# A transformer kernel: the four conditioning pieces of layer 1 that lay in norms, placed in the two projections

## Chip, cores and metric

The kernel runs on one NeuronCore of a Trainium2 chip. The metric is the time of one execution on the device in microseconds (us). The engines are TensorE (PE), VectorE (DVE), ScalarE (ACT), GpSimd (POOL) and SyncE (SP), which issues the weight transfers.

## The reference

Four layers over 256 tokens of width 1024, all in fp32. Layers 0 and 1 are conditioned: six vectors of 1024 per layer (shift, scale and gate of the mixer; shift, scale and gate of the feed-forward part) come from one product of the conditioning input with a weight of 1024 x 6144. Each is made for two streams, the latent tokens (`x`, conditioned by `c`) and the context tokens (`ctx`, conditioned by `c_ctx`):

```python
for l in range(DEPTH):
    mod = (jax.nn.silu(c) @ ada_w[l] + ada_b[l])[:, None, :]
    mod_c = (jax.nn.silu(c_ctx) @ ada_w[l] + ada_b[l])[None, None, :]
    sh1, sc1, g1, sh2, sc2, g2 = jnp.split(mod, 6, axis=-1)
    h = x * (1.0 + sc1) + sh1
    ...
    x = layer_norm(ALPHA * x + g1 * y, ln1_g[l], ln1_b[l])
    x = layer_norm(ALPHA * x + g2 * swiglu(x * (1.0 + sc2) + sh2, ffn_w_in[l], ffn_w_out[l]), ln2_g[l], ln2_b[l])
```

`y` is the mixer of the layer (attention and pooling in layer 0; differential attention and a convolution in layer 1). Layer 0 runs its output projection, norm, feed-forward part and second norm for both streams, layer 1 for the latent tokens alone. Layers 2 and 3 (mLSTM and RG-LRU mixers, cross attention, feed-forward with retrieved experts) have no conditioning and are not touched by the change.

## The kernel before

**Stages.** The program is a list of stages that all engines enter in turn: an engine leaves a stage with a drain and an increment, and `enter` waits until the others have left the stages before. For the conditioned layers the order is `ada0`, `modulate0`, `project0`, `attend0`, `pool`, then `out00`, `hidden00` (context) and `out01`, `hidden01` (latent), then `modulate1`, `project1`, `attend1`, `subln`, `out11`, `hidden11`. The `out` stages multiply by the output weight and end in a norm; the `hidden` stages are the feed-forward parts and end in a norm too. The hidden stages round their weights into a high and a low part (`w_split`, made by ACT at L1497 and DVE at L1887) and multiply three times.

**The ring.** All weights stream in blocks of 128 x 1024 fp32 (512 KB) through a ring of `R = 6` slots. `WEIGHTS` is the one list of the blocks in order; SP issues them (L531), waiting before block i until PE has used block i - 6 (`block_used`). A stage finds its blocks by `first_block`.

**A conditioning piece** is one of the six vectors of a layer, `KD = 8` blocks. `ada_block` (L698 to L704) multiplies a block: four matmuls of 32 columns, one for each quarter of the vector, side by side in the array; `ada_sum` is the bank in which a piece is summed, alternating between two. When the eight blocks of a piece are used, `keep_ada` on ACT (L1383 to L1386) copies the sum out, `ada_turn` on PE (L707 to L713) turns it into columns with two small matmuls, and `biased` on DVE (L1810 to L1822) adds the bias into `mod`, with 1 added to the two scale pieces. Before the first block of a piece, PE waits until the piece two before it is biased (`ada_out`), since the bank is the same.

**Where the pieces lie.** Pieces 0 and 1 of layer 0 are made in `ada0`. The projection puts conditioning blocks between its products: `ADA_AFTER[l][n]` says how many follow product n. In layer 0 that is three after each of ten products and two after the eleventh, the 32 blocks of pieces 2 to 5. In layer 1 it is one after each of the first 16 of 22 products, pieces 4 and 5. Pieces 0 to 3 of layer 1 are made in the norms at the end of `out00`, `hidden00`, `out01` and `hidden01`: there PE, after the matmuls for mean (L953) and variance (L959), runs the eight blocks of a piece (`ada_in_norm`, L715), while ACT and DVE finish the norm: root (L1389), reciprocal (L1685), scaling (L1861), shift (L1478) and, in the `out` stages, the modulated input of the hidden stage and its split (L1474, L1870, L1875). The piece is copied at the end of ACT's norm, turned between mean and variance of the next norm, and biased there by DVE; piece 3 is turned and biased at the head of `project1`.

**The projection** (`project_early`). PE runs for each n: product n (L806 and L809; 16 matmuls for 256 or 512 tokens, each counted as it appears in the trace), the conditioning blocks of n (L703), the turns of the pieces that were completed after product n - 1 (L712), and in layer 0 the head mean of n - 1 (L818) and the rotary partner of n - 2 (L829); in layer 1 the partner of n - 5, and two means for the convolution near the end (L836). ACT copies each product out and, in layer 0, squares it and takes the root; DVE normalizes and rotates in layer 0, and in layer 1 rotates and runs the 31 convolution taps. `BIASED_AT[l]` says after which of DVE's steps a piece is biased, and `pieces_after` when ACT copies one.

The expression that sets the mix of blocks in a projection (`project_weights`):

```python
for n in range(n_products):
    blocks.append((f"project{l}", tensor, 1, n))
    if ADA_AFTER[l][n]:
        blocks.append((f"project{l}", f"ada{l}", ADA_AFTER[l][n], at))
        at += ADA_AFTER[l][n]
```

Of the kernel before, what the change touches and what calls it, by code (L numbers as in the profile page):

```python
# [36 lines left out]
KD = D // P  # L37
# [24 lines left out]
QUARTER = D // 4  # L62
# [96 lines left out]
def project_weights(l, tensor, n_products):  # L159

    blocks, at = [], ADA_FIRST[l]
    for n in range(n_products):
        blocks.append((f"project{l}", tensor, 1, n))
        if ADA_AFTER[l][n]:
            blocks.append((f"project{l}", f"ada{l}", ADA_AFTER[l][n], at))
            at += ADA_AFTER[l][n]
    return blocks


ADA_AFTER = {0: [3] * 10 + [2, 0], 1: [1] * 16 + [0] * 6}  # L170
ADA_FIRST = {0: 2 * KD, 1: 4 * KD}
BIASED_AT = {0: {3: (2,), 6: (3,), 7: (4,)}, 1: {6: (4,), 11: (5,)}}
ADA_IN_NORM = ["out00", "hidden00", "out01", "hidden01"]
# [7 lines left out]
def pieces_after(l, n):  # L181
# [6 lines left out]
           ("out00", "ab_out", 8), ("ada1_0", "ada1", KD, 0), ("hidden00", "ffn0", 0), ("ada1_1", "ada1", KD, KD),  # L188
           ("out01", "ab_out", 8), ("ada1_2", "ada1", KD, 2 * KD), ("hidden01", "ffn0", 0), ("ada1_3", "ada1", KD, 3 * KD),
           ] + project_weights(1, "cd_in", 22) + [("out11", "cd_out", 8), ("hidden11", "ffn1", 0),  # L190
# [100 lines left out]
def program(nc, a, out, spread_rows):  # L291
    ctx = ExitStack()
    with ctx:
# [152 lines left out]

        def ada_sum(l, n):
            return ps[:, (2, 6)[l] + n % 2, 0:QUARTER]

        def ada_columns(l, n):  # L450
            return ps[:, (2, 6)[l] + n % 2, QUARTER:QUARTER + 2 * KD]
# [233 lines left out]
        def _(pe):  # L685
            place = RingPlace()
# [11 lines left out]
            def ada_block(l, n, k, blk):  # L698

                if k == 0 and n >= 2:  # L700
                    pe.wait_ge(ada_out, 6 * l + n - 1)
                for q in range(4):
                    last = mm(ada_sum(l, n)[32 * q:32 * (q + 1), :], cond_wide[:, k, :],  # L703
                              ring[:, blk[0], q * QUARTER:(q + 1) * QUARTER], start=(k == 0), stop=(k == KD - 1))  # L704
                last.then_inc(block_used, 1)
# [9 lines left out]

            def ada_in_norm(n):

                for k in range(KD):
                    place.steps(pe, 1, 1, lambda _, par, b: (wait_filled(b[0]), ada_block(1, n, k, b[0])))
# [70 lines left out]
            def project_early(l):  # L790
# [49 lines left out]
                if l == 1:  # L840
                    ada_turn(1, 3)
                turns = []
                for n in range(len(tiles)):
                    place.steps(pe, 1, 1, lambda _, par, b: product(n, b[0]))
                    at = ADA_FIRST[l] + sum(ADA_AFTER[l][:n])
                    for i in range(at, at + ADA_AFTER[l][n]):
                        place.steps(pe, 1, 1, lambda _, par, b: (wait_filled(b[0]), ada_block(l, i // KD, i % KD, b[0])))
                    for i in turns:
                        ada_turn(l, i)
# [98 lines left out]
            def norm(name):  # L948

                piece = ADA_IN_NORM.index(name) if name in ADA_IN_NORM else None  # L950
# [4 lines left out]
                if piece:  # L955
                    ada_turn(1, piece - 1)
# [6 lines left out]
                if piece is not None:  # L963
                    ada_in_norm(piece)
# [307 lines left out]
        def _(act):  # L1272
# [70 lines left out]
            def project_early(l):  # L1343
# [4 lines left out]
                for n, (j, _, nt, _) in enumerate(project_tiles(l)):  # L1348
# [22 lines left out]
                    for i in pieces_after(l, n):  # L1371
                        last = (i + 1) * KD - 1 - ADA_FIRST[l]
                        keep_ada(l, i, product_block(l, n) + 2 + last - sum(ADA_AFTER[l][:n]))
# [84 lines left out]
            def norm(name, s, ln, k12, follow=None):  # L1458
# [24 lines left out]
                if name in ADA_IN_NORM:  # L1483
                    n = ADA_IN_NORM.index(name)
                    keep_ada(1, n, first_block(f"ada1_{n}") + KD)
# [186 lines left out]
        def _(dve):  # L1672
# [37 lines left out]
            def project_early(l):  # L1710

                enter(dve, f"project{l}")
                if l == 1:
                    biased(1, 3)
                for i in range(len(ROPE[l])):
# [11 lines left out]
                    for n in BIASED_AT[l].get(i, ()):  # L1727
                        biased(l, n)
                if l == 0:
                    n_sq[0] += len(ROPE[0])  # L1730
                    rotate(l, len(ROPE[0]) - 1)
                    biased(0, 5)
# [116 lines left out]
            def norm(name, s, ln, k12, follow=None):  # L1849
# [6 lines left out]
                if name in ADA_IN_NORM[1:]:  # L1856
                    biased(1, ADA_IN_NORM.index(name) - 1)
# [615 lines left out]
```

## Time and profile before

| what | value |
|---|---|
| median of 3 runs | 3460.69 us |
| the runs | 3453.43, 3460.69, 3462.86 us |
| the profiled execution, its time | 3451.77 us |
| its span | 3450.1 us |
| mean granted clock of PE, of full speed | 0.96 |
| busy share PE, DVE, ACT, POOL | 92%, 60%, 36%, 3% |
| moved from memory | 543.92 MB read, mean 168 GB/s over the span |
| projection of layer 0, PE | 43.0 to 158.7 us |
| projection of layer 1, PE | 781.1 to 923.0 us |

The span is the time between first and last instruction in the trace; the execution's own time has 1.7 us more around it. In rows of the timeline the columns are start (us), length (us), engine, line, operation, output and inputs, count of merged instructions, and in brackets the idle time before and what ended it. Lengths of PE rows overlap slightly, so a piece of work is best measured from its start to the start of the next row. An fp32 matmul appears as two records.

### The profile page before, as it was taken

How to read it: one execution, taken by the hardware profiler on the slowest of the kernel's cores; microseconds unless marked ns; L12 is line 12 of the kernel's file. 1: busy time of each engine (PE TensorE's matmuls, PEld its weight loads, DVE VectorE, ACT ScalarE, POOL GpSimd, SP SyncE). 2: the span in 40 equal slices, each digit the busy share in tenths (PEclk: the TensorE clock that was granted, in tenths of full speed). 3: DMA queues.
4: the chain of work that ended last, by engine and by line, in shares of the span. 5: the costliest groups of instructions: out<-in, count | busy, mean ns of one | idle time of the engine just before them, and what ended most of it. 6: DMA issues, size and time to landing. Idle time of an engine off the chain costs nothing.

```text
span 3450.1 us, 52714 instructions
## 1 busy us (share of the span) xinstructions
PE 3162.0 (92%) x20312; PEld 2725.2 (79%) x20312; DVE 2083.7 (60%) x3709; ACT 1246.9 (36%) x1886; POOL 111.5 (3%) x135
## 2 busy tenths in 40 slices
PE   6978998999878999688999999999789899999998
PEld 2547987985758978477998999887678899999886
DVE  1474554553445540459995666784539996666686
ACT  1143443441224421122553444433422454444433
POOL 0110000000000000003000000000002100000000
PEclk9999999999989999799999999999889999999999
DMA  7504554545114533033556655674224466666663
GB/s 270 180 1 166 188 183 170 184 176 194 69 49 153 185 133 128 16 119 123 197 219 225 222 204 206 225 241 140 85 92 145 155 227 238 206 221 206 212 241 138
DMA packets 190525, 580.70 MB, mean 168 GB/s; under 512 B 16768, under 2 KB 61824, under 8 KB 185504
## 3 DMA queue, kind: packets, MB, share of 16 engines
q1 hardware_dynamic: 185120, 541.04, 44.9%
q10 hardware_dynamic: 4608, 33.56, 2.3%
q0 software_dynamic: 640, 4.00, 0.3%
q8 instruction: 101, 1.65, 0.2%
q14 instruction: 56, 0.46, 0.0%
HBM read 543.92 MB, written 34.60 MB: 168 GB/s over the span
## 4 chain that ended last, share of the span: by engine, by line
PE 82%; DVE 11%; ACT 4%; DMA 1%; issue 1%; DVEq 0%; ACTq 0%; SPq 0%; POOL 0%; POOLq 0%
PE ps L930 29%; PE ps L971 26%; PE ps L921 4%; PE ps L806 4%; PE ps L764 4%; PE ps L1172 3%; PE ps L809 2%; DVE w_split L2075 1%; PE ps L900 1%; PE ps L959 1%; ACT arena L1425 1%; PE ps L953 1%; PE ps L885 1%; DVE arena L1685 1%; PE ps L1137 1%
## 5 line engine op out<-in xcount | busy, mean ns | idle before, releaser
L930 PE MATMUL ps<-x_split,w_split 128*128 128x256 f32 x9312 | 1190.6, 286 | 72.5 <-DVE w_split L2075 39.8
L930 PEld LDWEIGHTS ps<-x_split,w_split 128*128 128x128 f32 x9312 | 1165.7, 194 | 97.0 <-issue 77.6
L971 PE MATMUL ps<-w_split,h_split 128*128 128x512 f32 x3864 | 916.6, 391 | 4.9 <-DVE w_split L2075 4.9
L971 PEld LDWEIGHTS ps<-w_split,h_split 128*128 128x128 f32 x3864 | 714.2, 189 | 146.4 <-issue 5.3
L2075 DVE TENSOR_TENSOR w_split<-ring,w_split 128x1024 fp32r<-128x1024 f32 x512 | 627.9, 1227 | 325.6 <-ACT w_split L1532 324.8
L1532 ACT ACTIVATE w_split<-ring 128x1024 fp32r<-128x1024 f32 x512 | 541.2, 1058 | 390.1 <-PE ps L971 352.1
L1887 DVE TENSOR_TENSOR w_split<-ring,w_split 128x1024 fp32r<-128x1024 f32 x198 | 242.3, 1226 | 237.8 <-ACT w_split L1497 237.8
L1497 ACT ACTIVATE w_split<-ring 128x1024 fp32r<-128x1024 f32 x198 | 209.1, 1059 | 330.4 <-PE ps L930 227.1
L1540 ACT ACTIVATE arena<-ps 128x256 f32<-128x256 f32 (+1 forms) x256 | 98.6, 385 | 460.8 <-PE ps L930 459.0
L921 PE MATMUL ps<-arena,ring 128*128 128x256 f32 (+1 forms) x672 | 154.1, 393 | 7.4 <-DVEq L1679 4.5
L806 PE MATMUL ps<-arena,ring 128*128 128x512 f32 (+1 forms) x416 | 154.8, 526 | 4.8 <-ACTq L1278 4.8
L921 PEld LDWEIGHTS ps<-arena,ring 128*128 128x128 f32 (+1 forms) x672 | 132.8, 199 | 29.1 <-issue 8.0
L764 PE MATMUL ps<-x,ring 128*128 128x256 f32 (+1 forms) x608 | 133.6, 382 | 6.3 <-ACTq L1278 6.3
L1137 PE MATMUL ps<-x,ring 128*128 128x256 f32 x512 | 119.6, 388 | 18.6 <-DVEq L1679 18.6
L806 PEld LDWEIGHTS ps<-arena,ring 128*128 128x128 f32 x416 | 81.0, 197 | 68.8 <-issue 63.7
L764 PEld LDWEIGHTS ps<-x,ring 128*128 128x128 f32 (+1 forms) x608 | 109.2, 180 | 30.1 <-issue 7.1
L1685 DVE RECIPROCAL arena<-arena 128x256 f32<-128x256 f32 (+2 forms) x26 | 63.1, 2429 | 108.7 <-ACT arena L1389 108.7
L1137 PEld LDWEIGHTS ps<-x,ring 128*128 128x128 f32 x512 | 97.4, 196 | 32.0 <-issue 19.4
L2204 DVE TENSOR_TENSOR h_split<-x,h_split 128x256 fp32r<-128x256 f32 x256 | 108.9, 425 | 8.8
L2197 DVE TENSOR_TENSOR x<-arena 128x256 f32<-128x256 f32 x256 | 107.5, 420 | 8.7 <-DMA arena<-spread_rows 8.7
L2180 DVE TENSOR_TENSOR arena<-arena,x 128x3072 bf16<-128x3072 bf16 x64 | 112.0, 1749 | 0.0
L1172 PE MATMUL ps<-res,arena 128*128 128x128 bf16 x1536 | 108.2, 227 | 0.4 <-DVE arena L2180 0.4
(264 smaller groups left out, 2439.4 us busy)
## 6 DMA issues: line engine op xcount, KB each, us to landing
ring<-in_peer_u SPq DMA_DIRECT2D x256, 512.0 KB, 3.5
ring<-in_peer_v SPq DMA_DIRECT2D x256, 512.0 KB, 4.3
ring<-in_ffn_in SPq DMA_DIRECT2D x132, 512.0 KB, 3.2
ring<-in_ada SPq DMA_DIRECT2D x96, 512.0 KB, 4.4
ring<-in_ffn_out SPq DMA_DIRECT2D x66, 512.0 KB, 3.2
spread_rows<-arena ACTq DMA_DIRECT2D x32, 1024.0 KB, 3.9
arena<-spread_rows SPq DMA_DIRECT2D x20, 1536.0 KB, 8.7
ring<-in_pq SPq DMA_DIRECT2D x32, 512.0 KB, 3.2
```

The lines of the kernel that those rows point to most:

```text
L764: last = mm(pair[0:width, par, 0:nt], w[:, k, :], src[:, k, t0:t0 + nt], start=(k == 0), stop=(k == KD - 1))
L806: last = mm(pair[:, n % 2, 0:nt], w[:, k, :], hT[:, k, t0:t0 + nt], start=(k == 0), stop=(k == KD - 1))
L921: last = mm(wide[:, m, :], ring[0:rows, blk[0], m * P:(m + 1) * P], rhs, start=(first and m % 2 == 0), stop=final, skip_group_check=True)
L930: last = mm(dst, w_split[:, w, wp, at:at + P], rhs[rp], start=(first and i == 0), stop=(final and i == 2), skip_group_check=shared)
L971: last = mm(ps[:, 2 * r + c, :], h_split[:, ph, hp, r * P:(r + 1) * P], w_split[:, b[3], wp, c * 512:(c + 1) * 512], start=(first and i == ...
L1137: last = mm(single[:, m % 2, 0:T], ring[:, b[0], k * P:(k + 1) * P], x[:, LAT, k, :], start=(k == 0), stop=(k == KD - 1))
L1172: last = mm(ps[:, bank, u * KEYS:(u + 1) * KEYS], hot_w[:, s % 2, c, :, 4 * half + u], hot_i[:, s % 2, 4 * half + u, :], start=(c == 0), s ...
L1497: f(w_split[:, w, 0, :], ring[:, slot, :], ACT.Copy).then_inc(w_high, 1)
L1532: f(w_split[:, w, 0, :], ring[:, slot, :], ACT.Copy).then_inc(w_high, 1)
L1887: v.tensor_tensor(w_split[:, w, 1, :], ring[:, slot, :], w_split[:, w, 0, :].bitcast(F32), ALU.subtract).then_inc(w_low, 1)
L2075: v.tensor_tensor(w_split[:, w, 1, :], ring[:, slot, :], w_split[:, w, 0, :].bitcast(F32), ALU.subtract).then_inc(w_low, 1)
L2180: v.tensor_tensor(hot_w[:, b], hot_j[:, b].unsqueeze(1).to_broadcast([P, 3, KEYS, GROUP]), weight3[:, :, at].unsqueeze(2).to_broadcast([P, ...
```

## The change

The list `ADA_AFTER` of layer 0 gets 48 blocks (four after each of eight products, then 5, 5 and 6), which are pieces 2 to 5 of layer 0 and pieces 0 and 1 of layer 1; that of layer 1 gets 32 (two after each of the first 16 products), pieces 2 to 5. Nothing of the conditioning stands in the norms any more, neither blocks nor turns, copies or biases. The number of blocks stays 96. Pieces 0 and 1 of layer 1 use banks 2 and 3, like those of layer 0; the later ones 6 and 7. `BIASED_AT` holds pieces numbered through both layers (layer 1 begins at 6) and gives their places on DVE; pieces 0 and 1 of layer 1 are biased at the end of the projection of layer 0.

```diff
--- before.py
+++ after.py
@@ -161,16 +161,16 @@
     blocks, at = [], ADA_FIRST[l]
     for n in range(n_products):
         blocks.append((f"project{l}", tensor, 1, n))
-        if ADA_AFTER[l][n]:
-            blocks.append((f"project{l}", f"ada{l}", ADA_AFTER[l][n], at))
-            at += ADA_AFTER[l][n]
+        for _ in range(ADA_AFTER[l][n]):
+            blocks.append((f"project{l}", f"ada{at // (6 * KD)}", 1, at % (6 * KD)))
+            at += 1
     return blocks
 
 
-ADA_AFTER = {0: [3] * 10 + [2, 0], 1: [1] * 16 + [0] * 6}
-ADA_FIRST = {0: 2 * KD, 1: 4 * KD}
-BIASED_AT = {0: {3: (2,), 6: (3,), 7: (4,)}, 1: {6: (4,), 11: (5,)}}
-ADA_IN_NORM = ["out00", "hidden00", "out01", "hidden01"]
+ADA_AFTER = {0: [4] * 8 + [5, 5, 6, 0], 1: [2] * 16 + [0] * 6}
+ADA_FIRST = {0: 2 * KD, 1: 8 * KD}
+BIASED_AT = {0: {1: 2, 3: 3, 5: 4, 7: 5}, 1: {0: 8, 3: 9, 7: 10, 11: 11}}
+
 
 
 def product_block(l, n):
@@ -185,9 +185,7 @@
 
 
 WEIGHTS = [("ada0", "ada0", 2 * KD, 0)] + project_weights(0, "ab_in", 12) + [
-           ("out00", "ab_out", 8), ("ada1_0", "ada1", KD, 0), ("hidden00", "ffn0", 0), ("ada1_1", "ada1", KD, KD),
-           ("out01", "ab_out", 8), ("ada1_2", "ada1", KD, 2 * KD), ("hidden01", "ffn0", 0), ("ada1_3", "ada1", KD, 3 * KD),
-           ] + project_weights(1, "cd_in", 22) + [("out11", "cd_out", 8), ("hidden11", "ffn1", 0),
+           ("out00", "ab_out", 8), ("hidden00", "ffn0", 0), ("out01", "ab_out", 8), ("hidden01", "ffn0", 0)] + project_weights(1, "cd_in", 22) + [("out11", "cd_out", 8), ("hidden11", "ffn1", 0),
            ("project2", "ml_in", 26), ("project2", "kv0", 4), ("out21", "ml_out", 8), ("hidden2", "peer0", 0),
            ("project3", "rg_in_r", 16), ("project3", "rg_in_q", 2), ("project3", "kv1", 4),
            ("out31", "rg_out_q", 2), ("out31", "rg_out_r", NRB), ("hidden3", "peer1", 0)]
@@ -444,11 +442,14 @@
         stored = sem("stored")
         bank_ready, rows_kept, back_ready = sem("bank_ready"), sem("rows_kept"), sem("back_ready")
 
+        def ada_bank(l, n):
+            return (6 if (l, n) >= (1, 2) else 2) + n % 2
+
         def ada_sum(l, n):
-            return ps[:, (2, 6)[l] + n % 2, 0:QUARTER]
+            return ps[:, ada_bank(l, n), 0:QUARTER]
 
         def ada_columns(l, n):
-            return ps[:, (2, 6)[l] + n % 2, QUARTER:QUARTER + 2 * KD]
+            return ps[:, ada_bank(l, n), QUARTER:QUARTER + 2 * KD]
 
         def rg_sum(g):
             bank = (0, 1, 2, 3, 6, 7, 0, 1)[g // 2]
@@ -697,7 +698,7 @@
 
             def ada_block(l, n, k, blk):
 
-                if k == 0 and n >= 2:
+                if k == 0:
                     pe.wait_ge(ada_out, 6 * l + n - 1)
                 for q in range(4):
                     last = mm(ada_sum(l, n)[32 * q:32 * (q + 1), :], cond_wide[:, k, :],
@@ -712,11 +713,6 @@
                     last = mm(ada_columns(l, n)[:, 8 * c:8 * (c + 1)], ada_row[:, at:at + P], const("pick"),
                               start=True, stop=True)
                 last.then_inc(ada_turned, 1)
-
-            def ada_in_norm(n):
-
-                for k in range(KD):
-                    place.steps(pe, 1, 1, lambda _, par, b: (wait_filled(b[0]), ada_block(1, n, k, b[0])))
 
             def ada(l):
 
@@ -837,16 +833,14 @@
                                   start=(k == 0), stop=(k == 1))
                     last.then_inc(conv_p, 1)
 
-                if l == 1:
-                    ada_turn(1, 3)
                 turns = []
                 for n in range(len(tiles)):
                     place.steps(pe, 1, 1, lambda _, par, b: product(n, b[0]))
                     at = ADA_FIRST[l] + sum(ADA_AFTER[l][:n])
                     for i in range(at, at + ADA_AFTER[l][n]):
-                        place.steps(pe, 1, 1, lambda _, par, b: (wait_filled(b[0]), ada_block(l, i // KD, i % KD, b[0])))
+                        place.steps(pe, 1, 1, lambda _, par, b: (wait_filled(b[0]), ada_block(i // (6 * KD), i // KD % 6, i % KD, b[0])))
                     for i in turns:
-                        ada_turn(l, i)
+                        ada_turn(i // 6, i % 6)
                     turns = pieces_after(l, n)
                     if l == 1 and n >= len(tiles) - 4 and n < len(tiles) - 2:
                         conv_mean(n - (len(tiles) - 4))
@@ -947,21 +941,16 @@
 
             def norm(name):
 
-                piece = ADA_IN_NORM.index(name) if name in ADA_IN_NORM else None
                 for k in range(KD):
                     pe.wait_ge(res_ready, KD * n_ln[0] + k + 1)
                     last = mm(pair[:, 0, 0:T], const("mean_d"), res[:, k, :], start=(k == 0), stop=(k == KD - 1))
                 last.then_inc(ln_mean, 1)
-                if piece:
-                    ada_turn(1, piece - 1)
                 for k in range(KD):
                     pe.wait_ge(ln_squared, 4 * n_ln[0] + k // 2 + 1)
                     last = mm(pair[:, 1, 0:T], const("mean_d"), work[:, k * T:(k + 1) * T],
                               start=(k == 0), stop=(k == KD - 1))
                 last.then_inc(ln_var, 1)
                 n_ln[0] += 1
-                if piece is not None:
-                    ada_in_norm(piece)
 
             def token_rows(ph, b, first, final):
 
@@ -1370,7 +1359,7 @@
                         root(work[:, 1024:1024 + T], ps[:, 3, 0:T], 0)
                     for i in pieces_after(l, n):
                         last = (i + 1) * KD - 1 - ADA_FIRST[l]
-                        keep_ada(l, i, product_block(l, n) + 2 + last - sum(ADA_AFTER[l][:n]))
+                        keep_ada(i // 6, i % 6, product_block(l, n) + 2 + last - sum(ADA_AFTER[l][:n]))
                 if l == 0:
                     n_sq[0] += len(ROPE[0])
                 leave()
@@ -1480,9 +1469,6 @@
                         high(k - 1)
                 if follow:
                     high(KD - 1)
-                if name in ADA_IN_NORM:
-                    n = ADA_IN_NORM.index(name)
-                    keep_ada(1, n, first_block(f"ada1_{n}") + KD)
                 n_ln[0] += 1
 
             def hidden(name, n, unit, after):
@@ -1710,8 +1696,6 @@
             def project_early(l):
 
                 enter(dve, f"project{l}")
-                if l == 1:
-                    biased(1, 3)
                 for i in range(len(ROPE[l])):
                     if l == 0:
                         t = proj[:, i, :]
@@ -1724,12 +1708,13 @@
                     else:
                         conv_taps(2 * i, 2 * i + 2)
                         rotate(l, i)
-                    for n in BIASED_AT[l].get(i, ()):
-                        biased(l, n)
+                    if i in BIASED_AT[l]:
+                        biased(BIASED_AT[l][i] // 6, BIASED_AT[l][i] % 6)
                 if l == 0:
                     n_sq[0] += len(ROPE[0])
                     rotate(l, len(ROPE[0]) - 1)
-                    biased(0, 5)
+                    biased(1, 0)
+                    biased(1, 1)
                 else:
                     conv_taps(2 * len(ROPE[1]), CONV)
 
@@ -1853,8 +1838,6 @@
                 for q in range(4):
                     two = res[:, 2 * q:2 * q + 2, :]
                     v.tensor_tensor(two, two, over(pair[:, 0, 0:T], 2), ALU.subtract).then_inc(ln_centred, 1)
-                if name in ADA_IN_NORM[1:]:
-                    biased(1, ADA_IN_NORM.index(name) - 1)
                 inverse_root(work[:, 4096:4096 + T])
                 dve.wait_ge(ln_centred, 4 * (n_ln[0] + 1))
                 for k in range(KD):
```

## Rows read from the trace of the kernel before

**Rows 1.** The page, part 4: the chain that ended last, by engine.
```profile
PE 82%; DVE 11%; ACT 4%; DMA 1%; issue 1%; DVEq 0%; ACTq 0%; SPq 0%; POOL 0%; POOLq 0%
```

**Rows 2.** Timeline, PE, projection of layer 0: start, length, line, operation, count.
```profile
61.59 1.50 PE L703 MATMUL ps<-ring,cond_wide 128*32 128x256 f32 x24
63.02 1.12 PE L818 MATMUL ps<-arena,consts 128*128 128x512 f32 x2
...
82.16 0.61 PE L712 MATMUL ps<-consts,arena 128*128 128x8 f32 x4
82.63 1.10 PE L818 MATMUL ps<-arena,consts 128*128 128x512 f32 x2
...
150.27 1.07 PE L703 MATMUL ps<-ring,cond_wide 128*32 128x256 f32 x16
151.27 7.13 PE L806 MATMUL ps<-arena,ring 128*128 128x512 f32 x16
```

**Rows 3.** Timeline, PE, projection of layer 1.
```profile
781.05 0.99 PE L712 MATMUL ps<-consts,arena 128*128 128x8 f32 x4 [5.06 <-ACTq L1278]
781.89 5.92 PE L806 MATMUL ps<-arena,ring 128*128 128x256 f32 x16
787.74 0.64 PE L703 MATMUL ps<-ring,cond_wide 128*32 128x256 f32 x8
788.31 3.72 PE L806 MATMUL ps<-arena,ring 128*128 128x256 f32 x16
791.96 0.64 PE L703 MATMUL ps<-ring,cond_wide 128*32 128x256 f32 x8
```

**Rows 4.** Timeline, PE, norms of out00 and of out11.
```profile
287.72 3.72 PE L959 MATMUL ps<-arena,consts 128*128 128x256 f32 x16 [1.52 <-ACT arena L1463]
...
306.54 3.76 PE L930 MATMUL ps<-x_split,w_split 128*128 128x256 f32 x16 [8.97 <-DVE w_split L1887]
...
1025.48 3.72 PE L959 MATMUL ps<-arena,consts 128*128 128x256 f32 x16 [1.52 <-ACT arena L1463]
1044.30 5.87 PE L930 MATMUL ps<-x_split,w_split 128*128 128x256 f32 x29 [15.10 <-DVE w_split L1887]
```

**Rows 5.** Timeline, PE and then ACT, norm of hidden00.
```profile
503.66 3.72 PE L959 MATMUL ps<-arena,consts 128*128 128x256 f32 x16 [1.10 <-ACT arena L1463]
...
512.63 0.64 PE L703 MATMUL ps<-ring,cond_wide 128*32 128x256 f32 x8 [0.75 <-DMA ring<-in_ada]
515.31 30.26 PE L921 MATMUL ps<-arena,ring 128*128 128x256 f32 x128 [2.04 <-DMA ring<-in_ab_out]
...
510.23 3.30 ACT L1478 ACTIVATE x<-res,params 128x256 f32<-128x256 f32 x8 [2.34 <-DVE res L1861]
513.44 0.36 ACT L1386 ACTIVATE arena<-ps 128x256 f32<-128x256 f32 x1
```

**Rows 6.** Timeline, PE, norm of hidden11 and the stage after it.
```profile
1241.20 3.72 PE L959 MATMUL ps<-arena,consts 128*128 128x256 f32 x16 [1.44 <-ACT arena L1463]
1251.21 8.44 PE L1041 MATMUL ps<-x,gate_w 128*4 128x256 f32 x32 [6.29 <-ACTq L1278]
```

**Rows 7.** Stretches (length, busy times, clock, DMA, GB/s); chain, out00 and out01.
```profile
512.60:513.30 0.70, 0.64 (x8) 0.16 (x8) 0.37 (x1) 0.70 (x3) 0.00 (x0) 1.00 1.00 357
...
514.00:515.30 1.30, 0.00 (x0) 0.02 (x1) 1.15 (x1) 0.00 (x0) 0.00 (x0) 0.50 1.02 410
...
254.88 27.86 PE ps L921 x128
...
515.31 30.26 PE ps L921 x128
```

**Rows 8.** Timeline, DVE, projection of layer 1: bias of a scale piece.
```profile
846.80 0.17 DVE L1821 TENSOR_SCALAR mod<-mod 128x16 f32<-128x16 f32 x1
```

**Rows 9.** Transfers into the ring, issue to landing: projection of layer 0, of layer 1.
```profile
DMA to landing us min/median/max: 3.2/5.4/7.9
...
DMA to landing us min/median/max: 3.2/4.0/5.1
```

## The prediction

> **What bounds the kernel now.** I read the chain of waits first: TensorE (PE) holds 82% of it [rows 1], so the question for each moved block is whether PE waits at the place that it leaves and at the place that it goes to. The timeline of PE in the projection of layer 0 [rows 2] has no idle time between the first product and the last (43.0 to 158.2 us; no row there has the bracket of an idle time): product, three conditioning blocks, mean, partner, next product, end to start. The same view of the projection of layer 1 [rows 3] shows the same from 781.9 to 923.0 us, a product and one block every 4.22 us (787.74 to 791.96) while the products have 256 columns. PE is the bound in both. In the norms it is not: in out00 the blocks end before 298 and PE then sits 8.97 us until DVE has split the first weights [rows 4]. Only after hidden00 does the next matmul wait for a transfer, 2.04 us [rows 5]. So the blocks leave places where PE waits and go to places where it does not.
>
> **What each norm gives back.** The norms of layer 1 have the same code without blocks, and are the measure.
> - out00 and out01: from the start of the variance matmuls to the first matmul of the hidden stage, 287.72 to 306.54 = 18.82 us with the blocks; out11 without them 1025.48 to 1044.30 = 18.82 us [rows 4]. Gain 0. What hides the blocks is the chain root, reciprocal, scaling, split on ACT and DVE; out01 (550.55 to 569.37 in the same view) agrees.
> - hidden00: 503.66 to 515.31 = 11.65 us [rows 5]; hidden11 without blocks 1241.20 to 1251.21 = 10.01 us [rows 6]. Gain 1.64 us. It has two parts: ACT's copy of the block sum (0.36 us, ends at 513.80; the copy before it ends at 513.53, so 0.27), and the transfer of the first output weight, which queued behind the eight conditioning blocks and is prefetched now.
> - hidden01: the same ACT copy goes from ahead of the modulation of layer 1: 0.27 us. PE waits there for ACT, not for a transfer. At the head of the projection the turn of piece 3 goes too, 781.05 to 781.89 = 0.84 us [rows 3]. That is at the slow clock, and the product behind it then takes more of the slow stretch, so between 0.42 and 0.84 comes back; I take 0.8, since the whole row goes.
> - The turns and biases that stood inside the norms were hidden beside ACT's square and root, and give 0.
>
> **The clock.** After the blocks of hidden00 the granted clock is 1.00 (2.4 GHz) until the last of them ends, then 0.50 (1.2 GHz) before the next stage begins, 2 us later; eight output weights then take 30.26 us, where out00, entered at the full clock, takes 27.86 [rows 7]. So a low-clock start costs 2.4 us and is paid already. hidden00 and hidden11 begin with PE busy for 19.88 and 19.66 us for their first 144 matmuls, after 9 and after 15 us of idling (chain of waits), so a longer pause costs no more. Further loss 0; bounds -2.4 (out01 happens to begin at the full clock) and +0.
>
> The Trainium skill, "TensorE: Matmul & The Clock Gate", section "Why this matters for your kernels", asks that no idle gaps stand between bursts of matmuls, since the clock falls back in them. By it the blocks are the filler that keeps the clock up, and taking them out would cost out01 one slow start, 2.4 us more, a sum of 18.5 in place of 16.1. The rows above disagree: with the filler in place the clock has fallen all the same.
>
> **What the projections pay.** PE's price of a block is read from starts: three blocks 61.59 to 63.02 = 1.43 us, two 150.27 to 151.27 = 1.00 [rows 2], one 787.74 to 788.31 = 0.57 [rows 3]. Each further block in a burst is 0.43 us, and all 32 join existing bursts.
> - Layer 0: 16 x 0.43 = 6.9. Six turns instead of four, each 82.16 to 82.63 = 0.46 [rows 2]: +0.9. The last bias is now that of a scale piece, with one more DVE operation of 0.17 us [rows 8] and its wait ahead of the attention: +0.2.
> - Layer 1: 16 x 0.43 = 6.9. Four turns in the stream for two: +0.9. Head of the stage, from above: -0.8 - 0.3.
> - Waits that move: a piece's first block waits for the bias of the piece two before. With the new list of biases DVE does each in the step in which the turn stands or one or two later, and the next user of that bank comes at least one product (about 7 us) behind; the closest is block 56 (piece 1 of layer 1) after product 9, behind the bias of piece 5 in DVE's step 7, with about 2.6 us to spare by the spacing of today's rows. Cost 0. ACT's copies of the sums sit behind copies that PE has already passed, 0.4 us each with ACT idle over 6 us a product.
>
> **The ring, layer 0.** Six slots: a block's load starts when the block six places before it is used. A load lands 3.2 us after issue at best, 5.4 in the median, 7.9 at worst in this projection [rows 9]; a lone block behind others adds 1.3 us (524 KB at the 410 GB/s of the norm's burst [rows 7]). Groups of five blocks reload in the 7 us of the product and need nothing until it is over. The last groups do not fit: after products 8 and 9 stand five conditioning blocks, after 10 six, so that product 10, the last block of group 10 and product 11 are loaded only during a burst. Burst of five: 5 x 0.43 + 0.14 = 2.3 us. Product 10: 3.2 - 2.3 - 0.5 (partner) = 0.4. Last block of group 10: 3.2 - 2.3 = 0.9. Product 11: issued 0.6 us behind that block's load and landing 1.3 behind it, 0.4. Sum 1.7 at best; by the median landing 3.1 + 2.6 + 0.5 + 1.2 (product 9) = 7.4. I take 2.5, nearer the low end, since the queue is almost empty when these loads start.
>
> **The ring, layer 1.** The first ten groups will be three blocks per 4.22 + 0.43 = 4.65 us, or 1.57 MB in 4.65 us = 338 GB/s, against 1.05 MB in 4.22 = 248 now. The queue has given 410 [rows 7], and loads there land after 3.2 to 5.1 us, median 4.0 [rows 9], where two groups ahead leaves a product 1.0 + 3.65 + 1.0 = 5.7 us. It fits narrowly. Low bound 0; high bound from layer 0, where four blocks take up to 7.9 us from the first issue (1.85 us a block): 3 x 1.85 = 5.55 a group, 0.9 x 10 = +9. I take 0.5.
>
> **Sum.** Layer 0: 6.9 + 0.9 + 0.2 + 2.5 = 10.5. Layer 1: 6.9 + 0.9 - 0.8 - 0.3 + 0.5 = 7.2. hidden00's norm: -1.6. Total +16.1 us. The profiled execution took 3451.8, so it becomes 3467.9; the median of the three runs is 3460.7 (3453.4 to 3462.9), 8.9 above the profiled one, and becomes **3476.8 us**, 0.47% slower. A measurement of this kernel can tell about 0.3% from no change, 10.4 us.
>
> **Rivals.**
> - *Transfers bound the projection of layer 1* (chance 0.15). Up to +9 there and the upper waits of layer 0 (+4.9): +30, 3490 us; half of it 3483. For: landing times of up to 7.9 us under bursts of four. Against: 410 GB/s seen in the norm, no PE wait on a transfer in either projection today.
> - *The cost stays under what can be told* (0.21). No ring wait in layer 1, 1.7 in layer 0, out01 at the full clock: 16.1 - 0.5 - 0.8 - 2.4 = +12.4; with a scatter of some 5 us in medians of three it can read +7 to +10, 3469 us. For: the spread of the three runs, 9.4 us. Against: the low-clock start is in the rows.
> - *Faster: the loads of the norms are on the path* (0.04). Eight blocks at 1.3 us are 10.2 us of the ring in each of four norms, ahead of the weights of the next stage. If that delayed every next stage, up to 4 x 10.2 = 41 would come back against 17.7 paid plus: 3437 us. It decides from 4.5 us a norm. For: out01's first weight did wait for it, 2.04 us. Against: 18.82 with and without blocks.
> - *The change is not what it says*: block counts are 48 and 32 in both lists, 96 in all as before, so every transfer and matmul is still done. No chance of its own.
>
> **Chances and range.** The forecast (+13 to +20) has 0.60, all of it slower; with the first rival slower is 0.75. Same 0.21, faster 0.04. Its own range is 3472 to 3482 with medians scattering; for 8 in 10 I go from 3466 (second rival) to 3489 (first rival).
>
> **What would show each step.** Right: PE's starts in the projection of layer 0 have bursts of four blocks 1.86 us long; idle time of PE with a ring transfer as releaser only after products 9 and 10; layer 1 groups 4.65 us apart; variance to next stage 18.8, 10.0 and 18.8 us in out00, hidden00, out01; both projections together about 18 us longer. Wrong: any idle time on a transfer in the first ten groups of layer 1, a hidden stage that begins sooner than 18.8 us after its variance, a clock of 1.00 at the start of out01, or bursts that cost less than 0.43 us a block.

## The result, and the profile after

| | before | after |
|---|---|---|
| median of 18 runs each | 3455.5 us (3452.1 to 3465.9) | 3470.6 us (3467.2 to 3485.4) |
| ratio, 95% interval | | 1.0042 [1.0033, 1.0051] |
| profiled execution, own time and span | 3451.8, 3450.1 us | 3474.5, 3472.8 us |

The change makes the kernel slower: the medians differ by 15.1 us, and the ratio of the runs gives 14.5 us (11 to 18 by its interval), against +16.1 predicted. The two profiled executions differ by 22.7 us, some 8 more. The stages say where, all read as differences of starts in PE's timeline:

| stretch, us | before | after | difference |
|---|---|---|---|
| projection of layer 0, first product to attention | 116.19 | 126.39 | +10.20 |
| attention of layer 0 and pooling | 95.66 | 101.76 | +6.10 |
| out00 and its norm, to hidden00 | 51.66 | 51.66 | 0 |
| variance of hidden00 to out01 | 11.65 | 10.01 | -1.64 |
| out01, to its variance | 35.24 | 34.32 | -0.92 |
| variance of out01 to hidden01 | 18.82 | 18.82 | 0 |
| variance of hidden01 to the projection of layer 1 | 14.55 | 14.28 | -0.27 |
| projection of layer 1, to attention | 142.75 | 150.01 | +7.26 |
| all the rest | 2963.6 | 2965.6 | +2.0 |

Four of these are the change: +10.20 - 1.64 - 0.27 + 7.26 = +15.55. The attention, which the change does not touch, is chance, as the last experiment shows, and so is the 0.92 of out01 (experiment 1).

First PE's timeline of the changed kernel in the projection of layer 0 (start, length, line, operation; in brackets the idle time and its releaser), which answers to [rows 2]:

```profile
52.71 1.93 PE L704 MATMUL ps<-ring,cond_wide 128*32 128x256 f32 x32
54.57 7.13 PE L802 MATMUL ps<-arena,ring 128*128 128x512 f32 x16
...
145.72 2.37 PE L704 MATMUL ps<-ring,cond_wide 128*32 128x256 f32 x40
148.02 0.70 PE L825 MATMUL ps<-arena,consts 128*128 128x256 f32 x2
149.21 7.13 PE L802 MATMUL ps<-arena,ring 128*128 128x512 f32 x16 [0.49 <-DMA ring<-in_ab_in]
156.27 2.37 PE L704 MATMUL ps<-ring,cond_wide 128*32 128x256 f32 x40
160.12 0.64 PE L704 MATMUL ps<-ring,cond_wide 128*32 128x256 f32 x8 [1.48 <-DMA ring<-in_ada]
160.69 0.61 PE L713 MATMUL ps<-consts,arena 128*128 128x8 f32 x4
161.36 7.13 PE L802 MATMUL ps<-arena,ring 128*128 128x512 f32 x16
...
169.50 1.14 PE L867 MATMUL ps<-arena 64*128 64x256 f32 x8 [0.67 <-DVEq L1665]
```

A burst of four blocks is 52.71 to 54.57 = 1.86 us; the three of [rows 2] took 1.43, so the added block is 0.43. In the tail PE waits for the ring at two places: 0.49 us for product 10, behind a burst of five, and 1.48 us for the sixth block of the last burst. The turn ahead of product 11 takes 160.69 to 161.36 = 0.67 in place of 0.46, which I read as a third wait of 0.2, although the row names no releaser.

The same view in the projection of layer 1, which answers to [rows 3]:

```profile
794.09 6.21 PE L802 MATMUL ps<-arena,ring 128*128 128x256 f32 x16 [10.56 <-ACTq L1267]
800.24 1.07 PE L704 MATMUL ps<-ring,cond_wide 128*32 128x256 f32 x16
801.24 3.72 PE L802 MATMUL ps<-arena,ring 128*128 128x256 f32 x16
804.89 1.07 PE L704 MATMUL ps<-ring,cond_wide 128*32 128x256 f32 x16
805.89 3.72 PE L802 MATMUL ps<-arena,ring 128*128 128x256 f32 x16
```

Groups are 800.24 to 804.89 = 4.65 us apart, with two blocks in 1.00, and no row of this projection names a transfer. But the ring is no longer at ease: its transfers land after

```profile
DMA to landing us min/median/max: 3.3/5.4/7.1
```

a median of 5.4 us (loads issued from 790 to 880 us), where [rows 9] had 4.0, and a load has 5.7 us. The 4.65 us hold for the groups without a rotary partner; from the sixth on a group has one and is 824.94 to 830.02 = 5.08 us long in the same timeline. So the queue is asked for 338 GB/s in the first five groups alone and for 1.57 MB in 5.08 us = 309 GB/s in the next five.

The norms, for [rows 4] and [rows 5], out00 and then hidden00:

```profile
304.10 3.72 PE L950 MATMUL ps<-arena,consts 128*128 128x256 f32 x16 [1.52 <-ACT arena L1452]
322.92 2.47 PE L924 MATMUL ps<-x_split,w_split 128*128 128x256 f32 x10 [15.10 <-DVE w_split L1870]
...
519.96 3.72 PE L950 MATMUL ps<-arena,consts 128*128 128x256 f32 x16 [1.44 <-ACT arena L1452]
529.97 20.28 PE L915 MATMUL ps<-arena,ring 128*128 128x256 f32 x86 [6.29 <-ACTq L1267]
```

PE idles 15.1 us now where it idled 8.97, and the hidden stage begins the same 18.82 us after the variance matmuls. After hidden00 the next stage begins 10.01 us after them, as [rows 6] had it, released by ACT leaving its stage and no longer by a transfer.

### The profile page after: what moved, and what is told of

Its sections match the earlier page's. It is cut to its first block, busy times and chain, and to the rows that moved or that the text cites. A ratio compares the mean times of both kernels' runs of the same rounds, so it can differ in the third digit from the quotient of the medians.

```text
span 3472.8 us, 52713 instructions
## 1 busy us (share of the span) xinstructions
PE 3171.5 (91%) x20312; PEld 2729.8 (79%) x20312; DVE 2082.6 (60%) x3709; ACT 1246.6 (36%) x1886; POOL 111.4 (3%) x135
## 3 DMA queue, kind: packets, MB, share of 16 engines
q8 instruction: 101, 1.65, 0.2%
## 4 chain that ended last, share of the span: by engine, by line
PE 82%; DVE 10%; ACT 4%; DMA 1%; issue 1%; ACTq 0%; DVEq 0%; SPq 0%; POOL 0%; POOLq 0%
PE ps L924 29%; PE ps L960 25%; PE ps L915 4%; PE ps L802 4%; PE ps L760 4%; PE ps L1161 3%; PE ps L805 2%; DVE w_split L2058 1%; PE ps L894 1%; PE ps L950 1%; PE ps L879 1%; ACT arena L1414 1%; PE ps L946 1%; DVE arena L1671 1%; PE ps L704 1%
## 5 line engine op out<-in xcount | busy, mean ns | idle before, releaser
L1126 PEld LDWEIGHTS ps<-x,ring 128*128 128x128 f32 x512 | 97.6, 196 | 32.1 <-issue 19.4
```

Of the source, the lines that this page charges most:

```text
L1126: last = mm(single[:, m % 2, 0:T], ring[:, b[0], k * P:(k + 1) * P], x[:, LAT, k, :], start=(k == 0), stop=(k == KD - 1))
```

## The experiments

In the table the two projections, the attention of layer 0 and the two norms that changed, from each kernel's profile, and the ratio to the kernel before with its interval. The projection of layer 0 is split: "first" is its first product, which begins at 1.2 GHz and takes 8.7 to 10.1 us as the clock rises sooner or later (0.50 until 49 us in the profile of before, 0.76 already from 45.2 to 47 us in that of "layer 1 half"); "rest 0" is all behind it, 106.07 us in each of the four profiles with the old list, so it can be read to a tenth.

| kernel | first | rest 0 | attention 0 | after hidden00 | after hidden01 | proj. 1 | ratio |
|---|---|---|---|---|---|---|---|
| before | 10.12 | 106.07 | 95.66 | 11.65 | 14.55 | 142.75 | 1 |
| after | 9.67 | 116.72 | 101.76 | 10.01 | 14.28 | 150.01 | 1.0042 |
| norms bare | 9.51 | 106.07 | 101.81 | 10.00 | 14.28 | 142.22 | 0.9988 [0.9979, 0.9997] |
| layer 0 half | 9.06 | 116.99 | 98.32 | 10.01 | 14.55 | 142.91 | 1.0024 [1.0013, 1.0035] |
| layer 1 half | 8.67 | 106.07 | 97.64 | 11.60 | 14.28 | 150.51 | 1.0023 [1.0012, 1.0033] |
| even bursts | 9.80 | 116.10 | 102.06 | 10.01 | 14.27 | 150.27 | 1.0053 [1.0040, 1.0067] |
| dense layer 1 | 8.68 | 116.57 | 98.33 | 10.01 | 14.28 | 160.05 | 1.0068 [1.0053, 1.0084] |
| one quarter | 9.23 | 116.64 | 98.56 | 10.01 | 14.27 | 150.57 | 1.0043 [1.0027, 1.0060] |
| fewer bursts | 9.25 | 105.46 | 99.75 | 11.14 | 14.55 | 138.74 | 0.9994 [0.9985, 1.0004] |
| fewer bursts, again | 9.79 | 105.46 | 95.85 | 11.76 | 14.54 | 138.74 | 0.9994 [0.9984, 1.0004] |
| wide products | 9.20 | 116.61 | 98.56 | 10.01 | 14.28 | 147.75 | 1.0041 [1.0026, 1.0055] |
| before, again | 9.11 | 106.07 | 104.62 | 11.75 | 14.55 | 142.76 | one run |

**1. The norms without their blocks.** The kernel before, with everything of the change's four pieces taken out of the norms and put nowhere:

```diff
-("out00", "ab_out", 8), ("ada1_0", "ada1", KD, 0), ("hidden00", "ffn0", 0), ("ada1_1", "ada1", KD, KD),
...
+("out00", "ab_out", 8), ("hidden00", "ffn0", 0), ("out01", "ab_out", 8), ("hidden01", "ffn0", 0)]
...
-ADA_IN_NORM = ["out00", "hidden00", "out01", "hidden01"]
+ADA_IN_NORM = []
...
+v.memset(mod[:, 1, 0:4 * KD, :], 0.5)
```

> The kernel before with the 32 conditioning blocks of the norms, their turns, copies and biases left out altogether (the four vectors are a constant 0.5 instead): what the norms give back, without what the projections pay. Theory (the norms hide their blocks): from the variance matmuls to the next stage 18.8 us in out00 and out01 as before, 10.0 after hidden00 (11.65 before), 14.3 after hidden01 (14.55), and the first product of layer 1 starts 0.84 us sooner; in all 2.7 us less than the kernel before, about 0.1%. Rival (the loads of the norms are on the path): 18.8 falls too, and the whole gains 10 us or more. Rival (the blocks keep the clock up): the first matmuls of the next stages take longer, and the gain is under 1 us or a loss.

PE's timeline in the norm of out00 and of hidden00:

```profile
293.47 3.72 PE L959 MATMUL ps<-arena,consts 128*128 128x256 f32 x16 [1.52 <-ACT arena L1463]
312.29 17.98 PE L930 MATMUL ps<-x_split,w_split 128*128 128x256 f32 x128 [15.10 <-DVE w_split L1885]
...
509.43 3.72 PE L959 MATMUL ps<-arena,consts 128*128 128x256 f32 x16 [1.44 <-ACT arena L1463]
519.43 15.80 PE L921 MATMUL ps<-arena,ring 128*128 128x256 f32 x65 [6.29 <-ACTq L1278]
```

18.82 and 10.00 us: the norms give back 1.65 (hidden00) + 0.27 (hidden01) and nothing else. At the head of the projection of layer 1 the missing turn brings 0.53 (142.75 to 142.22), not 0.84. In all 2.4 us by the stages; the ratio, 0.9988, is 4 us with an interval from 1 to 7. Beyond that place after hidden00 the loads of the norms are not on the path, though there were 32 of them fewer. The blocks are no filler for the clock either. Out01, to its variance, took 35.20 to 35.25 us in the five profiles with blocks in hidden00's norm. In the seven without them it took 34.32 (the changed kernel), 34.38 (here) and 34.44, or 35.76 to 35.84, on average 35.2. Each of the twelve begins it at a clock of 0.50. It is 1.00 from the fourth microsecond of the stage in the changed kernel, from the sixth in that of before, and still 0.50 in the sixth in "wide products". So without the blocks the clock rises sooner or later than with them, and on average nothing of the 2.4 us is lost. Why the stage is so steady with the blocks and not without them stays open.

**2. and 3. Each half alone.**

```diff
 # layer 0 half
+ADA_AFTER = {0: [4] * 8 + [5, 5, 6, 0], 1: [1] * 16 + [0] * 6}
+IN_NORM = {'out01': 2, 'hidden01': 3}
 # layer 1 half
+ADA_AFTER = {0: [3] * 10 + [2, 0], 1: [2] * 16 + [0] * 6}
+IN_NORM = {'out00': 0, 'hidden00': 1}
```

> Half of the change: pieces 0 and 1 of layer 1 go into the projection of layer 0 (48 blocks there, 4 x 8, 5, 5, 6), pieces 2 and 3 stay in the norms of out01 and hidden01, and the projection of layer 1 keeps its 16. Theory: projection of layer 0 from first product to the attention 126.4 us as in the changed kernel (116.2 before), with two waits for the ring of 0.5 and 1.5 us after products 9 and 10; the norm of hidden00 1.6 us shorter; projection of layer 1 as before, 142.8; in all +8.6 us, 0.25% slower. Rival (the attention of layer 0 is slower because of what precedes it, as it was by 6 us in the profiled execution of the change): +14 to +15 us, in the trace and in the median. If the 6 us are chance, the attention takes 95 to 102 us here and the median stays at +8.6.

> The other half: pieces 2 and 3 of layer 1 go into its projection (32 blocks, 2 after each of 16 products), pieces 0 and 1 stay in the norms of out00 and hidden00, the projection of layer 0 keeps its 32 blocks. Theory: projection of layer 1 150.0 us from its first matmul to the attention (142.8 before), its groups 4.65 us apart, no wait for the ring; projection of layer 0 116.2; the norm of hidden00 keeps its 11.65 us; hidden01's norm 0.27 us shorter; in all +7.0 us, 0.2% slower. Rival (transfers bound the dense groups): waits for the ring in the first ten groups and +10 us or more. With the other half it should add up to the change, +14 to +16.

Rest of the projection of layer 0 116.99 in the first, 106.07 in the second; projection of layer 1 142.91 and 150.51. The ratios give +8.3 and +7.9 us (8.6 and 7.0 expected), and 1.0024 and 1.0023 add up to the 1.0042 of the change within their intervals. The tail of the first half, by PE's timeline, has the waits of the changed kernel again:

```profile
148.43 7.13 PE L809 MATMUL ps<-arena,ring 128*128 128x512 f32 x16 [0.41 <-DMA ring<-in_ab_in]
...
159.67 0.64 PE L706 MATMUL ps<-ring,cond_wide 128*32 128x256 f32 x8 [1.76 <-DMA ring<-in_ada]
```

In the second, group 5 of layer 1 shows a first small wait for the ring, 0.18 us:

```profile
801.49 1.07 PE L706 MATMUL ps<-ring,cond_wide 128*32 128x256 f32 x16
802.74 3.72 PE L809 MATMUL ps<-arena,ring 128*128 128x256 f32 x16 [0.18 <-DMA ring<-in_cd_in]
```

The attention of layer 0 took 98.3 and 97.6 us, so the rival by which it is made slower by the projection ahead of it falls. Over all profiles its mean is 99.2 us in the six with 32 blocks in the projection ahead of it and 99.6 in the six with 48.

**4. The bursts of layer 0 spread evenly.**

```diff
-ADA_AFTER = {0: [4] * 8 + [5, 5, 6, 0], ...
+ADA_AFTER = {0: [4, 4, 5, 5, 5, 5, 4, 4, 4, 4, 4, 0], ...
```

> The changed kernel with the 48 blocks of the projection of layer 0 spread as 4, 4, 5, 5, 5, 5, 4, 4, 4, 4, 4, 0, so that no burst of five lacks the head mean behind it and none of six is left. Theory (the two waits at the end are the ring: a load that cannot start before the burst): both waits go, projection of layer 0 124.3 us (126.4 in the changed kernel), in all 2.1 us less than the changed kernel, +12 to +13 against the kernel before. Rival (the transfers are short of bandwidth in the whole projection): the waits move into the groups of five, and the 126.4 stays.

Missed. The waits at the end are gone, and two others stand behind bursts of five:

```profile
82.84 2.37 PE L704 MATMUL ps<-ring,cond_wide 128*32 128x256 f32 x40
...
87.42 7.13 PE L802 MATMUL ps<-arena,ring 128*128 128x512 f32 x16 [0.72 <-DMA ring<-in_ab_in]
...
110.21 7.13 PE L802 MATMUL ps<-arena,ring 128*128 128x512 f32 x16 [0.78 <-DMA ring<-in_ab_in]
```

Rest 0 is 116.10 against 116.72: 0.6 us won, not 2.1, and the ratio shows none of it. Behind a burst of five the next product lies in the slot of the one before, so its load begins when that product ends, here at 82.8, and lands at 87.4, 4.6 us later. Between them stand burst, mean and partner, 3.9 us to the end of the partner. Behind the other two bursts of five a turn (0.46) stands there too, and the loads, which landed 3.8 and 3.7 us after issue where these two took 4.4 and 4.5, were in time. Six slots with a period of six leave no room. No burst of four in layer 0 has such a wait in any profile, so what matters is the length of the burst and not only its place; 48 blocks behind eleven products cannot all be in bursts of four, and a list without a wait was not tried.

**5. The ring of layer 1 loaded beyond what it gives.**

```diff
-... 1: [2] * 16 + [0] * 6}
+... 1: [4] * 8 + [0] * 14}
```

with the first two biases at the head of the stage, since PE's later blocks wait for them.

> The changed kernel with the 32 blocks of the projection of layer 1 after its first eight products, four each, where a product has only 256 columns: a group is five blocks (2.62 MB) in 3.65 + 1.86 = 5.5 us of TensorE, 476 GB/s, more than the queue has delivered. Theory (at 410 GB/s, 1.28 us a block): groups 6.4 us apart, 0.9 us of waiting for the ring in each of some seven, less 8 x 0.14 for bursts saved: the projection about 155 us (150.0 in the changed kernel). Rival (bursts of transfers get only 1.85 us a block, as the landings in layer 0 suggest): groups 9.2 us apart, the projection 175 us.

PE's timeline for one group:

```profile
814.85 3.70 PE L802 MATMUL ps<-arena,ring 128*128 128x256 f32 x16
818.48 1.07 PE L704 MATMUL ps<-ring,cond_wide 128*32 128x256 f32 x16
819.86 0.64 PE L704 MATMUL ps<-ring,cond_wide 128*32 128x256 f32 x8 [0.31 <-DMA ring<-in_ada]
821.22 0.64 PE L704 MATMUL ps<-ring,cond_wide 128*32 128x256 f32 x8 [0.72 <-DMA ring<-in_ada]
822.50 3.72 PE L802 MATMUL ps<-arena,ring 128*128 128x256 f32 x16 [0.64 <-DMA ring<-in_cd_in]
...
830.25 3.72 PE L802 MATMUL ps<-arena,ring 128*128 128x256 f32 x16
```

Between both theories and nearer the first: groups 7.65 and 7.75 us apart, the stage 160.05. That is 1.53 us a block, 343 GB/s, less than the 410 of a short burst and more than the 283 of 1.85 us a block. PE's waits name the ring eleven times, 6.6 us in sum. Part of the rest is the clock, which fell twice between the pauses (the product at 807 took 5.3 us for 3.7); in stretches of this kernel (length, busy times, clock, DMA share, GB/s):

```profile
805.00:812.00 7.00, 5.73 (x31) 4.06 (x24) 0.00 (x0) 0.38 (x1) 0.00 (x0) 0.76 1.03 416
...
820.00:830.00 10.00, 7.51 (x68) 4.30 (x62) 0.00 (x0) 1.67 (x4) 0.00 (x0) 1.00 1.01 390
...
840.00:850.00 10.00, 8.49 (x56) 5.80 (x55) 2.85 (x7) 0.38 (x1) 0.00 (x0) 0.83 0.98 364
```

The changed kernel asks 338 GB/s in its first five groups. That is 1% below the average of the two groups above; but the stretches of the same trace reached 416 and 390 GB/s, so 343 is no ceiling that this run shows. That little is to spare in those groups is shown by the waits of 0.18 and 0.19 us that "layer 1 half" and "one quarter" have at group 5.

**6. One matmul of four in a block.** Three quarters of the last four vectors of layer 1 are left out; the transfers stay.

```diff
-for q in range(4):
+for q in range(4 if l == 0 or n < 2 else 1):
```

> The changed kernel with one of the four 32-column matmuls of each of the 32 conditioning blocks in the projection of layer 1 (three quarters of four vectors are left out), all transfers kept. Theory (the four run side by side in the array, so a block costs what one of them costs): a further block in a burst stays at 0.43 us, and the projection at 150.0 us. Rival (the price goes with the number of matmuls): 0.11 us a further block, and the projection about 10 us shorter, 140 us.

```profile
803.45 1.05 PE L704 MATMUL ps<-ring,cond_wide 128*32 128x256 f32 x4
804.43 3.72 PE L802 MATMUL ps<-arena,ring 128*128 128x256 f32 x16
```

Two blocks take 0.98 us with 4 records as they took 1.00 with 16, and the stage 150.57. The four matmuls of 32 columns do run side by side: a block costs what one of them costs, and leaving the others out does not cut it.

**7. and 8. Fewer bursts in the kernel before.**

```diff
-ADA_AFTER = {0: [3] * 10 + [2, 0], 1: [1] * 16 + [0] * 6}
+ADA_AFTER = {0: [4] * 8 + [0] * 4, 1: [0] * 10 + [4] * 4 + [0] * 8}
```

> The kernel before (blocks in the norms) with the same blocks of the projections in fewer bursts: layer 0 four after each of eight products in place of three after ten and two, layer 1 four after each of products 10 to 13 in place of one after each of sixteen. Theory (a burst costs 0.14 us beside its blocks): layer 0 3 x 0.14 = 0.4 less, and no turn and bias at its end, 0.5 to 0.9 less: 115.0 us (116.2 before); layer 1 12 x 0.14 = 1.7 less: 141.1 us (142.8); in all 2.5 to 3 us less than the kernel before, 0.08%. Rival (bursts of four in layer 1 wait for the ring or for the bias): no gain there.

> The same kernel as e6_fewer_bursts once more, since its stages say 5.5 us less than the kernel before (0.16%) and its first measurement, 0.9994 with an interval to 1.0004, does not settle the sign. If the stages are right: projection of layer 0 114.7, of layer 1 138.7 us again, and a ratio near 0.9984. If the gain is given back elsewhere: a stage behind it that is longer in both profiles, and a ratio near 1.

Rest 0 is 105.46 in both profiles, 0.6 us less (0.9 to 1.3 expected). Layer 1 gave 4.0 us, not 1.7, in both. PE's timeline where no burst stands any more:

```profile
810.48 0.59 PE L829 MATMUL ps<-arena,consts 128*128 128x256 f32 x2
810.91 3.62 PE L806 MATMUL ps<-arena,ring 128*128 128x256 f32 x16
814.37 0.59 PE L829 MATMUL ps<-arena,consts 128*128 128x256 f32 x2
```

Partner to partner 3.89 us. With one block between, the kernel before has 4.65 (809.41 to 814.06). The difference is 0.76 us for the first block of a burst, not 0.57: the product behind it and the partner are about 0.1 longer each. So a burst costs 0.33 beside its blocks, and twelve fewer give 4.0. In layer 0 the three bursts fewer gave about 0.9 by the same timeline; but the fourth turn now stands in the stream and costs 0.46, while the end of the stage (last product to attention, 7.95 us before) became only 0.2 shorter, where 0.5 to 0.9 was expected.

The whole gained less than its stages. Twice 0.9994, with intervals to 1.0004: 2 us, and no sign that can be told. The attention of layer 1 took 68.6 us in both profiles against 66.9 in that of before, but 68.2 in the second of before, so this is not shown to be an answer to the edit. Whether this kernel beats the one before stays open; it is not slower.

**9. Fewer bursts in the changed kernel.**

```diff
-... 1: [2] * 16 + [0] * 6}
+... 1: [0] * 10 + [4] * 8 + [0] * 4}
```

> The changed kernel with the 32 blocks of the projection of layer 1 moved to where a product has 512 columns: four after each of products 10 to 17, none after the first ten. Two theories of what a burst costs beside 0.43 us a block. By the 0.14 that the prediction used (one block 0.57, two 1.00): 8 bursts fewer, the projection 150.0 - 1.1 = 148.9 us. By what the fewer bursts of the kernel before showed (12 bursts fewer gave 4.0 us, so 0.33 each, since the product and the partner behind a burst are longer too): 150.0 - 2.6 = 147.4 us. No wait for the ring in either, since a group of five has 8.8 us. In all +11 to +12 us against the kernel before.

147.75 us, 2.6 below the mean of the changed lists (150.34): the 0.33 holds for this edit as well. The ratio, 1.0041, is that of the changed kernel; 2.3 us are below what it tells.

**10. The kernel before once more.**

> The kernel before, unchanged, profiled a second time, for the attention of layer 0: 95.7 us in its first profile, 101.8 in that of the change, with the clock at 1.2 GHz for 15 us more. If that is chance: the projections 116.2 and 142.8 us again to within 1 us and the attention anywhere between 95 and 102. If the code ahead of it sets it: 95.7 again to within half a us.

Projections 115.18 and 142.76; attention 104.62 us, nine more than in the first profile, and the span 3463.4 against 3450.1. One stretch of 30 us in it, by length, busy times and clock, in the first profile of before:

```profile
175.20:205.20 30.00, 21.56 (x170) 12.15 (x168) 25.36 (x63) 16.19 (x63) 6.57 (x7) 1.00 0.00 1
```

in that of after:

```profile
185.50:215.50 30.00, 26.78 (x144) 15.09 (x143) 21.07 (x54) 13.59 (x54) 6.55 (x7) 0.61 0.00 1
```

and in the second of before:

```profile
174.20:204.20 30.00, 26.25 (x149) 14.80 (x149) 22.00 (x56) 13.80 (x55) 6.69 (x8) 0.67 0.00 1
```

The clock is 1.00 in the first, 0.61 and 0.67 in the others. DVE did 63 operations in it in the first and 54 and 56 in the others: the stage goes at PE's pace when the clock is low, with PE busy for 26.8 and 26.3 of the 30 us there and for 21.6 in the first. With the same code, from one execution to the next, this stage takes 95.7 to 104.6 us. It is chance, and nine of the 17 us over which the runs of before spread (3448.8 to 3465.9) can come from it alone.

## Why the prediction was right

- **The norms.** 0 in out00 and out01, -1.64 after hidden00, -0.27 after hidden01: all as predicted, to 0.01 us. The norms of layer 1, same code without the blocks, were the right measure.
- **PE's price.** 0.43 us a block in every burst of the trace, 13.8 for the 32, and the one-quarter run shows what it consists of.
- **The projection of layer 0.** Predicted +10.5. The two profiles differ by 10.20, but that holds the luck of the first product. Rest 0 is 106.07 in all four profiles with the old list and 116.72, 116.99, 116.57, 116.64 and 116.61 with the new one: +10.6. Of it 6.9 + 0.9 + 0.2 + 2.2 = 10.2 is in the rows named above, and 0.4 more around the waits: product 10 takes 7.06 us for 6.96, the partner ahead of it 0.70 for 0.54, and the last block 0.57 for 0.43.
- **The ring in it.** 2.5 taken, 0.49 + 1.48 + 0.2 = 2.2 measured. The three places were named with 0.4, 0.9 and 0.4 at best. The sixth block waited longer than that: its load was issued at 156.37 us, 0.1 after product 10, and took 3.7 us where the sum has 3.2. The place of the cost was right. Its size was a choice between 1.7 and 7.4 and not worked out, so that it came within 0.3 is in part luck. The step to experiment 4 was too mild: its expectation took 3.9 us between one product and the next as enough, and there the next product's load was ready only after 4.6. The transfers issued between 155 and 161 us for the sixth block and product 11 (size, median time to landing):

```profile
ring<-in_ada SPq DMA_DIRECT2D x1, 512.0 KB, 3.7
ring<-in_ab_in SPq DMA_DIRECT2D x1, 512.0 KB, 4.3
```

- **The projection of layer 1.** Predicted +7.5 without the 0.3 that stands in the norm. Measured 7.26; the means over three profiles with one block a group and four with two are 142.81 and 150.34, +7.5. Inside it the head turn was over-sized, 0.8 for 0.53, and 0.5 of waiting was 0.0 to 0.2; the two misses nearly cancel, which is luck.
- **The sum.** With these means in place of single profiles the stages add up to 10.6 - 1.6 - 0.3 + 7.5 = +16.2 us, inside the interval of 11 to 18.
- **The clock.** No further loss. The advice of the Trainium skill against idle gaps ("TensorE: Matmul & The Clock Gate", section "Why this matters for your kernels"), read as a reason to keep the blocks as filler, did not bear here: the norm without blocks cost out01 nothing on average (experiment 1).
- **The rivals.** Transfers did not bound layer 1, though with little to spare in five groups (experiment 5). The upper bound of that rival used 1.85 us a block, which does not follow from its own row: four blocks in 7.9 us are 1.98 each; the groups of experiment 5 took 1.53. The loads of the norms were off the path but for the 1.64 us after hidden00 that the sum has (experiment 1). The smaller cost that could not be told would have needed out01 at the full clock, which no profile had at its start.
- **The time.** 3476.8 was the median of three runs plus 16.1; with 18 runs the median of before is 3455.5, 5 us lower, and 3470.6 is 15.1 above it. The step on which the absolute number was 6 us high is the baseline, not the sum. For the same reason 3470.6 lies below the forecast's own range of 3472 to 3482 and next to the 3469 of the second rival; the stages speak against that rival all the same.

## What to carry to other kernels

Work that sits where its engine waits for others costs nothing, and its price elsewhere is read from the trace: here 0.43 us a block on PE, with four matmuls side by side or one, plus 0.33 for each place at which a product stream is broken. A twin stage without the work (here the norms of the next layer) tells what taking it out can give, to a hundredth. With a ring of n slots, count the blocks between a load's slot coming free and its use: a burst that, with its product, fills the ring leaves the next product's load only the time of the burst to land in, and what is missing is waited for.

## What was not expected

- The attention of layer 0 takes 95.7 to 104.6 us in executions of the same code, by the clock that PE is granted in its first 45 us. Two profiled executions cannot be compared by their spans here, only stage by stage.
- A lone conditioning block between two products costs 0.76 us, though the next row starts 0.57 after it: what follows it is slower by 0.2.
- Blocks of 512 KB came at 410 GB/s in a short burst [rows 7], and at 343 GB/s on average through two groups of experiment 5, while the three stretches shown there moved 364 to 416 GB/s with the DMA engines busy all the time (shares of 0.98 to 1.03).
